# Thirteen more products without a consumer on TensorE, at three places of a two-model kernel

## What is computed

```python
def first_block(x, c, ...):
    mod = silu(c) @ w_ada + b_ada                      # shift1 scale1 gate1 shift2 scale2 gate2
    h = modulate(rms_norm(x, g_norm1), shift1, scale1)
    proj = h @ w_in
    ...                                                # 8 heads of stick-breaking, 4 of gated linear attention
    x = x + (1 + gate1) * (mixed @ w_out)
    h2 = modulate(rms_norm(x, g_norm2), shift2, scale2)
    u = causal_depthwise_conv(h2 @ w_up, w_conv, b_conv)
    x = x + (1 + gate2) * ((val * silu(gte)) @ w_down)
    return rms_norm(x, g_final)

def second_block(x, mem, positions, ...):              # two layers
    # layer A: RWKV-7 mixing and 4 heads of attention to a memory, then SwiGLU
    # layer B: 12 causal heads with latent keys and values, 4 heads to the memory, then SwiGLU
    ...
    return rms_norm(x, final_norm_g)
```

## Time and profile before

| | |
|---|---|
| median of three executions | 1083.9 us |
| lowest, highest | 1081.49, 1085.06 us |
| span of the profiled execution | 1082.7 us |
| TensorE busy | 1042.9 us (96%) |
| mean granted clock of TensorE | 0.985 |
| VectorE busy, ScalarE busy | 734.7, 562.1 us |
| chain that ended last: TensorE's share | 88% |

### The profile page before, as it was taken

One profiled execution on the slowest core, in us unless ns is written; L12 is line 12 of the kernel. 1 busy time (PEld: TensorE's weight loads), 2 busy tenths in 40 slices (PEclk: granted clock), 3 DMA queues, 4 the chain that ended last, 5 costly groups with the idle time before them and its releaser, 6 DMA issues.

```text
span 1082.7 us, 22912 instructions
## 1 busy us (share of the span) xinstructions
PE 1042.9 (96%) x9968; PEld 988.3 (91%) x9968; DVE 734.7 (68%) x1194; ACT 562.1 (52%) x858; POOL 0.9 (0%) x7
## 2 busy tenths in 40 slices
PE   7999999899999999998899999999999999999997
PEld 6798898899999998887779999999989799999996
DVE  3788658799976667887546566566757665556554
ACT  4446374666556448754236444454667655444431
POOL 0000000000000000000000000000000000000000
PEclk8999999899999999999999999999999999999999
DMA  9968455466645653331005555456224435554441
GB/s 348 393 216 312 176 195 204 153 228 237 232 148 176 220 224 118 118 118 42 4 2 170 196 187 187 140 182 222 100 74 155 175 119 195 188 183 149 173 166 39
DMA packets 31236, 185.82 MB, mean 172 GB/s; under 512 B 3472, under 2 KB 4768, under 8 KB 13984
## 3 DMA queue, kind: packets, MB, share of 16 engines
q1 hardware_dynamic: 31136, 184.36, 47.4%
HBM read 183.29 MB, written 1.05 MB: 170 GB/s over the span
## 4 chain that ended last, share of the span: by engine, by line
PE 88%; DVE 5%; ACT 3%; DMA 2%; issue 1%; SPq 1%; DVEq 0%; ACTq 0%
PE banks L361 48%; PE banks L1354 17%; PE banks L341 5%; PE banks L358 2%; PE banks L637 2%; DMA land<-in_mkv_a 1%; DVE wlo L321 1%; PE banks L1538 1%; PE banks L1897 1%; PE banks L1887 1%; PE banks L572 1%; DVE adac L556 1%; PE banks L640 1%; PE banks L1864 1%; DMA raw<-in_w_in 1%
## 5 line engine op out<-in xcount | busy, mean ns | idle before, releaser
L321 DVE TENSOR_TENSOR wlo<-raw,whi 128x2048 fp32r<-128x2048 f32 (+3 forms) x163 | 323.1, 1983 | 172.5 <-ACT whi L306 171.7
L306 ACT ACTIVATE whi<-raw 128x2048 fp32r<-128x2048 f32 (+3 forms) x163 | 270.5, 1661 | 109.3 <-PE banks L1354 78.0
L361 PE MATMUL banks<-h_hi,whi 128*128 128x256 f32 x1376 | 181.1, 283 | 1.3 <-ACT h_hi L987 1.2
L361 PE MATMUL banks<-h_lo,whi 128*128 128x256 f32 x1376 | 179.2, 281 | 0.7 <-DVE h_lo L1062 0.7
L361 PE MATMUL banks<-h_hi,wlo 128*128 128x256 f32 x1376 | 177.4, 281 | 0.0
L361 PEld LDWEIGHTS banks<-h_hi,whi 128*128 128x128 f32 x1376 | 169.1, 189 | 4.7 <-issue 2.5
L361 PEld LDWEIGHTS banks<-h_lo,whi 128*128 128x128 f32 x1376 | 167.4, 187 | 4.1 <-issue 2.6
L361 PEld LDWEIGHTS banks<-h_hi,wlo 128*128 128x128 f32 x1376 | 167.8, 188 | 1.6 <-issue 1.2
L1380 ACT ACTIVATE u<-u 128x256 f32<-128x256 f32 x44 | 18.4, 418 | 128.9 <-DVE u L1434 128.8
L1354 PE MATMUL banks<-m_lo,whi 128*128 128x256 f32 x528 | 75.4, 281 | 0.0
L1354 PE MATMUL banks<-m_hi,wlo 128*128 128x256 f32 x528 | 75.3, 281 | 0.0
(11 more groups left out here) (449 smaller groups left out, 1405.2 us busy)
## 6 DMA issues: line engine op xcount, KB each, us to landing
raw<-in_ada SPq DMA_DIRECT2D x24, 1024.0 KB, 6.2
raw<-in_w_up SPq DMA_DIRECT2D x22, 1024.0 KB, 4.8
raw<-in_a_gu SPq DMA_DIRECT2D x22, 1024.0 KB, 4.8
raw<-in_b_gu SPq DMA_DIRECT2D x22, 1024.0 KB, 4.9
raw<-in_w_in SPq DMA_DIRECT2D x12, 1024.0 KB, 7.1
raw<-in_w_down SPq DMA_DIRECT2D x16, 704.0 KB, 4.1
raw<-in_a_in SPq DMA_DIRECT2D x11, 1024.0 KB, 5.6
raw<-in_a_down SPq DMA_DIRECT2D x16, 704.0 KB, 4.1
```

The lines of the kernel that those rows point to most:

```text
L306: act.activation(hi_s[k % NSPLIT][:, 0:w], raw[n % NRAW][:, 0:w], ACT.Copy).then_inc(*hi_made.tick(k))
L321: dve.tensor_tensor(lo_s[s][:, 0:w], raw[n % NRAW][:, 0:w], hi_s[s][:, 0:w].bitcast(F), SUB).then_inc(*lo_made.tick(k))
L361: i_ = pe.matmul(b[0:m, j * T:(j + 1) * T], a[:, kt * step + j * m:kt * step + j * m + m], x[:, kt, :], start=st, stop=sp)
```

## The change

A helper `pe_spin(pe, b, n)` multiplies `rmask` by itself n times into bank b, where no engine reads the result, with no wait and no semaphore update. `pe_wake` now calls it. It is called at four more points: 2 products at place 1, between the last sum and the first projection; 3 ahead of the mean and 4 behind it at place 2; 2 at place 3, between the values of head 12 and the transposes of head 13. Nothing is removed or moved. The banks that they write (4, 5, and 2, which is `sbank`) are idle at that time.

```diff
+        def pe_spin(pe, b, n):
+
+            for _ in range(n):
+                pe.matmul(b[:, 0:T], rmask[:, 0:P], rmask[:, 0:T], start=True, stop=True)
+
         def pe_wake(pe):
 
             pe.wait_ge(*misc_pool.at("rmask"))
-            for n in range(5):
-                pe.matmul(bank[0][:, 0:T], rmask[:, 0:P], rmask[:, 0:T], start=True, stop=True)
+            pe_spin(pe, bank[0], 5)
...
                 for n, _ in enumerate(pe_mkv(pe, c)):
                     pe_extra(pe, c, n)
+            pe_spin(pe, bank[4], 2)
             two = [pe_own(pe, NM), pe_own(pe, NM + 1)]
...
             if up == "w_up":
+                pe_spin(pe, bank[5], 3)
                 pe_mean(pe, before, bank[4])
+                pe_spin(pe, bank[5], 4)
...
             values(12)
+            pe_spin(pe, sbank, 2)
             turn(13)
```

## The result

| | before | after |
|---|---|---|
| median, first comparison (19 executions each) | 1083.95 us | 1081.45 us |
| lowest to highest | 1080.89 to 1088.38 | 1077.87 to 1084.92 |
| ratio, 95% interval | | 0.9973 (0.9960 to 0.9985) |
| the changed kernel a second time | 1084.2 (35) | 1079.53 (12), ratio 0.9961 (0.9946 to 0.9976) |
| and a third time | 1084.36 (20) | 1079.31 (12), ratio 0.9960 (0.9947 to 0.9973) |

A forecast was written before the change was run, and what follows sets the result against it. TensorE, busy 96% of the span, was taken as the bound, winnable where it waits or runs slowly. Places 1 to 3 sum 0 + 2.5 + 1.5 = 4.0 us, typically 3.1; forecast 3.5, hence 1080.4 us, range 1078.4 to 1083.0.

The forecast's parts named there:

- The price of a filler: On TensorE, one added product takes 0.45 us at full clock and 0.89 us at low clock; the full-clock price was taken.
- Place 1 is worth nothing: Ahead of the first projection, two products fit the wait; gain 0, since TensorE waits for VectorE's last h_lo tiles.
- Place 2: Around the mean behind w_out, seven products avoid the low clock; 2.5 us in the profiled execution, typically 2.0.
- Place 3: Ahead of head 13's transposes, two products avoid the low clock; 1.5 us in the profiled execution.
- The other term: At place 3 the drop may not come in some executions; gain 0 to 1.7 us, middle 1.1.
- B: Place 3's clock still drops and only place 2 gives, 2.0 to 2.5 us: 1081.4 to 1081.9 us; chance 0.16.
- D: Fillers run at low clock and delay the work at all three places, 3.6 us slower: 1087.5 us; chance 0.07.
- C: Nothing measurable: the clock falls despite place 2's fillers, or another engine takes the lead back; 1083.9 us; chance 0.05.
- A: The drops of places 2 and 3 both go, mostly 2.3 to 4.3 us: 1079.6 to 1081.6 us; chance 0.72.
- the moment: When TensorE's clock falls and rises is not fixed by the program; so a typical gain of 3.1 us, without it 4.0.

The follow-up runs named there:

- the doubled series: The changed kernel with six and eight products at place 2 and the calls of places 1 and 3 out; 14.40 us over place 2.
- p1_fed: The changed kernel with seven half-width products added between the first eight projections and the calls of places 2 and 3 out; one execution of 1081.85 us.
- p3_only: The changed kernel with the calls of places 1 and 2 out, only place 3's two products kept; 1081.66 us, ratio 0.9981 (0.9965 to 0.9997).
- p3_turns: The kernel before with eight transposes of rmask at place 3, where the change has two products; 11.37 us over place 3.
- p2_only: The changed kernel with the calls of places 1 and 3 out, only place 2's seven products kept; 1082.84 us, ratio 0.9985 (0.9966 to 1.0005).

## Why the prediction was right

It said 1080.4 us, 1078.4 to 1083.0. The first comparison gave 1081.45, the later ones 1079.5 and 1079.3. It gave "faster by over 0.3%" and "within 0.3%" about the same chance, and the three ratios lie on both sides of that line.

- **The price of a filler** was taken as 0.45 us at full clock. Measured: three in 1.46 us from first start to last end, four in 1.89, which is 0.22 from pass to pass and 0.43 a product. Both series ended ahead of the work behind them. The price was slightly too high, as the doubled series shows (0.95 us where 1.1 were worked out, 1.78 where 2.3 were).
- **Place 1 is worth nothing:** right, and for the reason given. The clock fell behind the paced stretch instead of ahead of it, and VectorE's last `h_lo` tile decided. p1_fed, at full clock up to there, started the 25 products 13.77 us behind the first projection as well.
- **Place 2:** 2.5 us forecast, 2.40 measured in the profiled execution, and 2.2 on average over six profiles without fillers (14.77 - 12.53). One step was named wrongly: the prediction has VectorE's last `h_lo` as what ends the stretch, at 201.6. By its own figures TensorE is later: the 32 products end at 199.9, and sixteen more at some 0.12 us each end at 201.8, which would have given 2.4. In the trace after, that tile is ready at 197.49 + 3.25 = 200.74, while the sixteen products with `h_lo` run from 199.30 to 201.16 without a wait. TensorE's own 48 products end last (5.67 us from 195.49). The two chains lie within half a microsecond of each other, so the number came out all the same; that much is luck.
- **Place 3:** 1.5 us forecast for an execution in which the clock had fallen, 1.61 measured. The other term was the size over all executions, "0 to 1.7, middle 1.1". It is not settled. The clock fell in two of eight profiles without a filler, which makes 0.4 us on average, but eight are few: p3_only was 0.3 to 3.8 us faster, and its executions had 5.0 us less low clock. A single profile that shows a drop does not say how often it comes.
- **Rivals.** B (place 3 still drops) and D (the fillers run at low clock) did not occur. C (nothing measurable) falls by the three ratios, all below 1 with their intervals. A (both drops go) is what all four profiles with the whole change show, the one with further fillers included. Of the moment, the traces show this: the kernel before, profiled twice, fell near place 2 and again at 505.1 and 860.1 in one execution, and near place 2 and at neither of the others in the second. Near place 2 the fall came 5.0 to 5.6 us behind w_out's last sixteen in five profiles and lasted 6.8 us, and 7.9 us behind and lasted 3.4 in p3_turns, where the stretch took 14.05 us and not 14.8 to 15.1. With this agrees what the Trainium skill says ("TensorE: Matmul & The Clock Gate", Part 1), that the gate's decision runs free of the kernel's start.
- **What no term of the sum held** is the pace of dense products. It took 1.39 us back in the profiled execution. p3_turns, which has the slow pace without place 2's fillers, and p2_only, which has the fast one with them, show that the fillers are not its cause.

The forecast's average of 3.1 us was made of 2.0 and 1.1; averages over the 14 profiles give 2.2 + 0.4 = 2.6. The first comparison's 2.9 (1.6 to 4.3, from the interval of the ratio) agrees. The two later ones, 4.2 and 4.3, are above it, with lower ends at 2.6 and 2.9. The low clock that the two places do not explain (3 to 6 us of it, above) is a candidate for the rest, at no more than half a microsecond each; but the kernel with twelve more fillers had less low clock for the same time. Near 66, 88 and 126 to 129 us the clock fell in 3 of 10 profiles of kernels with only part of the change or none, and in 0 of 4 with all of it, which is too few to tell. Why the later comparisons gave more, and what sets the pace, is open.

## What to carry to other kernels

A product without a consumer is free as long as it ends before the awaited result is there. Fit the number to the wait at full clock; 0.2 to 0.4 us to spare were enough here. Before filling a wait, ask who is last behind it: at place 1 another engine was, and a full clock was worth nothing. Profile the unchanged kernel several times before you price a drop of the clock, since one that is seen once may be there in one execution out of four. And prefer a place whose drop is in every profile of the unfilled kernel, as place 2's was.

## What was not expected of the hardware

- In dense series of equal products at full clock the step from product to product takes one of a few fixed values for tens of microseconds: 117.3, 118.7 or 120.0 ns in the first `w_down` (528 products), 116.7 or 117.8 ns in `w_up`. It differs between executions of one program (118.7 and 120.0 in `w_down`, 116.7 and 117.8 in `w_up` for the changed kernel). From the second chunk of `w_up` to the end of `w_down` it makes 181.4 to 183.4 us over all profiles, 182.0 to 183.4 within the changed kernel.
- Executions of the same kernel spread over 9.7 us (1079.56 to 1089.22 for the kernel before in one comparison). Falls of the clock at stretches where it does not always fall, 1.5 to 2.1 us each (near 88, 127, 129 and at place 3), and this pace are two parts of it that the profiles show. A third is larger: from the end of the first `w_down` to place 3 the 14 profiles took 467.3 to 471.7 us, on average 1.7 us more in the four whose clock fell near 504 than in the others; the rest of that spread has no explanation here.
- A later rise of the clock at the start was not worse. In the two fastest starts (first projection at 48.4 and 48.8 us) it rose only at 11.0 and 10.4 us and then did not fall near 17; in the twelve others it rose at 4.4 to 7.7, fell at 16 to 19, and the first projection came at 49.8 to 51.6.
